# Triangular inverse of the RWKV recurrence: levels 1 to 5 over the 32 columns that each level changes

## What is computed

```python
def step(state, inp):
    r_t, w_t, k_t, v_t, kk_t, a_t = inp
    sk = jnp.einsum('bhij,bhj->bhi', state, kk_t)
    state = (state * w_t[:, :, None, :]
             - sk[..., None] * (kk_t * a_t)[:, :, None, :]
             + v_t[..., None] * k_t[:, :, None, :])
    y = jnp.einsum('bhij,bhj->bhi', state, r_t)
    return state, y
```

## Time and profile before

| | us |
|---|---|
| median of 3 runs | 3304.61 |
| the runs | 3301.97 to 3306.84 |
| the profiled execution | 3303.65 |
| its span, first to last instruction | 3301.9 |
| the stretch of the recurrence's levels in it | 1830.9 to 2411 |
| TensorE busy, whole span | 2822.2 (85%) |
| VectorE busy | 1513.9 (46%) |
| GpSimd busy | 1480.1 (45%) |
| ScalarE busy | 912.5 (28%) |

### The profile page before, as it was taken

The page is one execution under the profiler, slowest core; times in us unless marked ns, Lnnn a source line. Parts: engine busy times, 40 slices in busy tenths (PEclk is TensorE's granted clock), DMA queues, the critical chain, the costliest instruction groups (busy, mean ns, idle before and its releaser), DMA issues. The chain is left out here.

```text
span 3301.9 us, 59409 instructions
## 1 busy us (share of the span) xinstructions
PE 2822.2 (85%) x25224; PEld 2310.6 (70%) x25224; DVE 1513.9 (46%) x1839; ACT 912.5 (28%) x1616; POOL 1480.1 (45%) x817
## 2 busy tenths in 40 slices
PE   2788889999999994999644888888839999999999
PEld 1565667888888872777423778888738788878887
DVE  6744655655443445222342555555532544434434
ACT  2434433222222212222232333333322422222221
POOL 2533244444444442555442566555615544444443
PEclk9889989999999996999867999999969999999999
DMA  6512252545333320555324111111133232333233
GB/s 219 178 51 64 58 166 83 199 159 191 106 95 97 96 80 29 125 133 127 96 64 99 54 54 48 48 60 51 38 84 90 83 99 93 102 90 101 90 102 121
DMA packets 207762, 323.85 MB, mean 98 GB/s; under 512 B 126112, under 2 KB 126240, under 8 KB 207520
## 3 DMA queue, kind: packets, MB, share of 16 engines
q1 hardware_dynamic: 107680, 295.12, 29.1%
q10 hardware_dynamic: 99840, 25.17, 3.4%
HBM read 285.71 MB, written 33.55 MB: 97 GB/s over the span
## 5 line engine op out<-in xcount | busy, mean ns | idle before, releaser
L652 POOL TENSOR_TENSOR wl<-w,wh 128x1024 fp32r<-128x1024 f32 x320 | 782.2, 2450 | 1142.9 <-ACT wh L688 1142.6
L213 PE MATMUL ps<-hi,wh 128*128 128x512 f32 x1824 | 729.7, 400 | 58.7 <-POOL wl L652 43.9
L214 PE MATMUL ps<-lo,wh 128*128 128x512 f32 x1824 | 716.5, 393 | 0.0
L215 PE MATMUL ps<-hi,wl 128*128 128x512 f32 x1824 | 716.3, 393 | 0.0
L688 ACT ACTIVATE wh<-w 128x1024 fp32r<-128x1024 f32 x320 | 338.1, 1058 | 728.6 <-DMA w<-in_ffn_w_in 551.2
L899 DVE SCALAR_TENSOR_TENSOR xt<-ps,mod,xt 128x512 f32<-128x512 f32 x384 | 286.4, 750 | 429.8 <-PE ps L215 429.8
L213 PEld LDWEIGHTS ps<-hi,wh 128*128 128x128 f32 x1824 | 346.5, 190 | 144.5 <-POOL wl L652 44.1
L215 PEld LDWEIGHTS ps<-hi,wl 128*128 128x128 f32 x1824 | 346.1, 190 | 74.2
L214 PEld LDWEIGHTS ps<-lo,wh 128*128 128x128 f32 x1824 | 346.6, 190 | 73.4 <-issue 3.3
L213 PE MATMUL ps<-act_hi,wh 128*128 128x512 f32 x704 | 278.9, 396 | 11.4 <-DVE act_lo L908 10.2
L215 PE MATMUL ps<-act_hi,wl 128*128 128x512 f32 x704 | 277.7, 394 | 0.0
(11 more groups left out here) (214 smaller groups left out, 4537.6 us busy)
## 6 DMA issues: line engine op xcount, KB each, us to landing
w<-in_ffn_w_in SPq DMA_DIRECT2D x176, 512.0 KB, 3.7
piece<-in_ada_w SPq DMA_DIRECT2D x96, 512.0 KB, 4.8
w<-in_ffn_w_out SPq DMA_DIRECT2D x88, 512.0 KB, 3.6
w_raw<-in_w_rkv SPq DMA_DIRECT2D x48, 512.0 KB, 4.0
scratch<-stage ACTq DMA_DIRECT2D x96, 256.0 KB, 2.4
w<-in_wqk SPq DMA_DIRECT2D x20, 512.0 KB, 5.1
xt<-in_xT SPq DMA_DIRECT2D x4, 2048.0 KB, 12.1
w<-in_attn_w_out SPq DMA_DIRECT2D x16, 512.0 KB, 3.7
```

Source lines behind the costliest of these rows:

```text
L213: pe.matmul(out, w_hi(k), x_hi(k), start=first and k == 0, stop=False)
L214: pe.matmul(out, w_hi(k), x_lo(k), start=False, stop=False)
L215: ins = pe.matmul(out, w_lo(k), x_hi(k), start=False, stop=last and k == kc - 1)
L652: pool.tensor_tensor(wl[n % NW][:, :, :], wr[n % NW][:, :, :], wh[n % NW][:, :, :].bitcast(F32), ALU.subtract).then_inc(*wlo.up)
```

## The change

At level l with n = LEVELS[l], the product of `level_x` changes only the even blocks of n columns of each 64 (`blocks(.., l, 0)`), and the transpose only the odd ones (`blocks(.., l, 1)`): 32 columns either way. The moving operand, the output of each product, the sum and the two copies of levels 1 to 5 now go over these 32 columns. The stationary operands stay 64 x 64. The number of instructions in the levels and their order on each engine stay the same. Runs of neighbouring columns are 2 long at level 1, then 4, 8, 16 and 32.

So that the odd columns of `one_plus_x` are right without being written, each level has a tile of its own, filled with the identity once before the first period. Level 0 stays full and writes its sum to `inv`, where level 1 reads it.

```diff
-                wx, tinv = st("one_plus_x"), st("inv")
+                wx, tinv = [None] + [st(f"one_plus_x{l}") for l in range(1, len(LEVELS))], st("inv")
...
+                def blocks(x, l, odd):
+
+                    return x.rearrange("p a (g t n) -> p a g t n", t=2, n=LEVELS[l])[:, :, :, odd, :]
+
+                def merged(x):
+
+                    return x.rearrange("p a g n -> p (a g) n")
...
                             if l < NL - 1:
-                                act.activation(tinv[:, pairs, :], quarter(q), ACT.Copy)
-                            act.activation(inv[b][:, pairs, :], quarter(2 + q), ACT.Copy).then_inc(*g["t_done"].up)
+                                act.activation(merged(blocks(tinv[:, pairs, :], l, 0)), merged(blocks(quarter(q), l, 0)), ACT.Copy)
+                            act.activation(merged(blocks(inv[b][:, pairs, :], l, 1)), merged(blocks(quarter(2 + q), l, 1)), ACT.Copy).then_inc(*g["t_done"].up)
...
-                                    ins = pe.matmul(quarter(q)[hs, j, :], ntm[l % 2][hs, jj, :],
-                                                    idst[hs] if l == 0 else (wx if l == 1 else tinv)[hs, jj, :], start=True, stop=True)
+                                    if l == 0:
+                                        ins = pe.matmul(quarter(q)[hs, j, :], ntm[0][hs, jj, :], idst[hs], start=True, stop=True)
+                                    else:
+                                        ins = pe.matmul(blocks(quarter(q), l, 0)[hs, j], ntm[l % 2][hs, jj, :],
+                                                        blocks(tinv, l, 0)[hs, jj], start=True, stop=True)
...
                                     if l < NL - 1:
-                                        pe.matmul(quarter(q)[hs, j, :], inv[b][hs, jj, :], wx[hs, jj, :], start=True, stop=True)
+                                        pe.matmul(blocks(quarter(q), l, 0)[hs, j], inv[b][hs, jj, :], blocks(wx[l], l, 0)[hs, jj],
+                                                  start=True, stop=True)
...
-                                    ins = pe.matmul(quarter(2 + q)[hs, j, :], wx[hs, jj, :], inv[b][hs, jj, :],
+                                    ins = pe.matmul(blocks(quarter(2 + q), l, 1)[hs, j], wx[l][hs, jj, :], blocks(inv[b], l, 1)[hs, jj],
                                                     start=True, stop=True)
...
-                            dve.tensor_tensor(wx[:, pairs, :], quarter(q), idst.unsqueeze(1).to_broadcast([P, QP, CHUNK]),
-                                              ALU.add).then_inc(*g["w_done"].up)
+                            one = idst.unsqueeze(1).to_broadcast([P, QP, CHUNK])
+                            if l == 0:
+                                dve.tensor_tensor(tinv[:, pairs, :], quarter(q), one, ALU.add).then_inc(*g["w_done"].up)
+                            else:
+                                dve.tensor_tensor(blocks(wx[l][:, pairs, :], l, 0), blocks(quarter(q), l, 0), blocks(one, l, 0),
+                                                  ALU.add).then_inc(*g["w_done"].up)
...
                         dve.wait_ge(*g["zeros"].at(1))
+                        for x in wx[1:]:
+                            dve.tensor_copy(x[:, :, :], idst.unsqueeze(1).to_broadcast(W8)).then_inc(*g["wx_set"].up)
+                        dve.wait_ge(*g["wx_set"].at(NL - 1))
                         dve.wait_ge(*reset_in.at(1))
```

More of the change, by code:

```diff
@@ L94 @@
 wkv_s_done wkv_y_done_w wkv_m_step wkv_yc_done wkv_ysq_done wkv_var_done wkv_yrt_done wkv_yrn_done
-wkv_ybd_done wkv_yf_done wkv_z1_done wkv_bias_done wkv_z_step wkv_zeros g_in0*16 g_in1*16
+wkv_ybd_done wkv_yf_done wkv_z1_done wkv_bias_done wkv_z_step wkv_zeros wkv_wx_set g_in0*16 g_in1*16
 chunk_used0 chunk_used1 post_done0 post_done1 z_stored*16 z_in0*16 z_in1*16 z_hi z_lo stored*16
@@ L1318, in wkv_phase @@
                          "m_step yc_done ysq_done var_done yrt_done yrn_done ybd_done yf_done z1_done bias_done z_step "
-                         "zeros").split()
+                         "zeros wx_set").split()
                 g = {n: sig("wkv_" + n, 16 if n in ("tiles_in", "v_in") else 1) for n in names}
```

## The result

The changed kernel takes 3330.77 us (median of 4 runs, 3328.69 to 3332.42), against 3303.67 for the kernel before in the same comparison: ratio 1.0081, 95% interval 1.0063 to 1.0098. It is slower by 27 us. The forecast was 3298.6, the range 3288 to 3306.5.

The account below looks back on a forecast made before the run. TensorE's path with its waits for VectorE and GpSimd was taken to bound the recurrence; 0.303 us a period over 14 chunks (4.2), plus 0.7 and 1.1 for chunks 0 and 15, saved 6.0 us: 3298.6 us, range 3288 to 3306.5.

Parts of the forecast that it names:

- What bounds the kernel: Recurrence, TensorE 87% busy: the path of the 37.49 us period holds two VectorE sums and no ScalarE copy.
- the two sums that were named: VectorE's sums of levels 3 and 5, on the path: gains of 0.138 and 0.165 us a period.
- Part 1, the pace of TensorE: Matmuls of levels 1 to 5: a pair stays at 0.0587 us with 32 moving columns; only a batch's end 27 ns earlier.
- Part 2, the sums: VectorE sums of levels 1 to 5: each saves 0.138 us, ten a period, two of them on the path.
- Part 3, the copies: ScalarE copies, eighteen a period: each saves 0.107 us, counting only where a period lacks the work that hides them.
- Part 4, the fill: Filling tiles at the start: five VectorE copies, 3.5 us at most, hidden in 6.5 us of DMA wait, costing nothing.
- The sum: Whole recurrence: 4.2 us saved in chunks 1 to 14, 0.7 in chunk 0, 1.1 in chunk 15, total 6.0 us.
- the last rival: Recurrence: clock falls to 1.2 GHz as fewer columns move; a third of the stretch costs some 100 us; chance 0.03.

Follow-up runs that it names:

- e5: Changed kernel with all 64 columns in the products of levels 1 to 5, in jumping order (even blocks, then odd): 3304.06 us, ratio 1.0001.
- e12: As e10 (32 columns, waits filled), but the filling at level 3 is two matmuls of 128 x 192 for 128 x 256: 3299.65 us, ratio 0.9982.
- e10: Changed kernel, 32 columns, with unread matmuls filling TensorE's waits at levels 1, 2 and 3: 3301.79 us, ratio 0.9995.
- e11: As e10, same filling at levels 1, 2 and 3, but all 64 columns in the products: 3302.19 us, ratio 0.9999.
- e1: Changed kernel with all 64 columns in the products of levels 1 to 5, sums and copies at 32: 3302.07 us, ratio 0.9995.
- e9: Changed kernel with 64 columns in the products and 96 extra elements summed ahead of each sum, restoring the old period: 3303.28 us, ratio 0.9999.
- e7: Changed kernel with 64 columns in the products and unread matmuls filling the waits ahead of levels 1 and 2: 3300.01 us, ratio 0.9987.
- e3: Changed kernel with all 64 columns in the products of level 1 alone, levels 2 to 5 at 32: 3311.99 us, ratio 1.002.
- e6: Changed kernel, 32 columns, with unread matmuls filling the waits ahead of levels 1 and 2: 3315.17 us, ratio 1.0033.
- e2: Changed kernel, 32 columns, with 96 extra elements summed on VectorE ahead of each sum, restoring the old period: 3317.64 us, ratio 1.0048.
- e8: Kernel before the change, with unread matmuls filling the waits ahead of levels 1 and 2: 3304.26 us, ratio 1.0000.

## Why the prediction was wrong

- *What bounds the kernel*: right for a period at full clock. Ordinary periods take 37.17 us for the 37.19 forecast, through the two sums that were named: t3 starts 0.13 us earlier behind `state_products`, and `gram` k 0.16 earlier behind x5. Only the wait ahead of `gram` k was misread, forecast to shrink to 0.35 and measured at 0.54, since t5 ahead of it moved by about the same 0.16.
- *Part 1, the pace of TensorE*: right in an undisturbed period. Batches of 16 narrowed instructions start 0.46 to 0.47 us apart, 0.058 to 0.059 a pair, as forecast; in e5 jumps cost nothing. The Trainium skill ("Advanced Engine Details and Errata", "PSUM Cachelines") states that any non-contiguous PSUM pattern slows matmuls, beside asking that every two consecutive elements be neighbours. The first does not show here, neither at runs of 2 columns (1.15 us in e5) nor longer; the second was kept in every run and is not tested.
- *Part 2, the sums*: L1801 takes 282 ns for the 276 forecast. *Part 3, the copies*: 275 and 280 ns for 272 to 278. *Part 4, the fill*: hidden, and 1.77 us long for a bound of 3.5.
- *The sum*: 4.9 of the 6.0 us were for chunks 0 to 14. With the clock up, e12, the kernel of the forecast but for the filling, gives 5.7 us less over the levels, 0.3 in each period from chunk 1 on, as forecast, and 1.4 in chunk 0 (0.7 forecast). Part of the 1.4 is luck that the sum did not have, the order of VectorE and GpSimd shown under e10 and e11. In its median e12 is 4.4 us below the kernel before.
- *The step that failed* is that the sum took the granted clock as 1.00 in every period after the change too, and put its fall at nothing outside the last rival, "the clock falls, as fewer columns move", with a chance of 0.03. I read the 1.00 of the earlier trace rows as a state with room to spare, although the same rows showed TensorE stopping for 1.86 us in every period. It had none: e1 shows that 0.3 us off the period are enough, with every column still moving. In its place the runs showed a clock at half for 82 of the 573 us of the levels, which made them 19.9 us longer where 4.9 less were forecast. The rival's price was wrong too, "some 100 us": it took a third of the stretch for this, and a fall costs half its length less what the waits behind it give back, 4.2 us for the two of a slow period at 32 columns and 0.3 for the one at 64.
- The mechanism that I named for it was half of it. Shown by the pairs of runs: the moment at which the waits come (e1 against e9, at 64 columns); the waits themselves (e1 against e7, the changed kernel against e12); the number of columns, which makes a fall behind mask 1 10.2 us for 3.4 (the changed kernel against e1 and e3) and lets a 0.80 us wait start one (e3 and e6 against e1). What decides whether a given wait brings a fall stays open (in e1 the same wait brings none in chunks 2, 3 and 6); so does why e2 differs from run to run by 17 us.
- The Trainium skill ("TensorE: Matmul & The Clock Gate", section "Loop structure matters more than you think") ties a cold clock to loop nests in which long waits stand between the matmuls. In these traces one loop nest is at either level, and falls begin behind waits of 1.85 and of 0.80 us; where the two differ, the measurement decides.

## What to carry to other kernels

A granted clock of 1.00 in a stretch where TensorE stops again and again (here for 1.85, 1.33 and 0.80 us in each period) can be lost by a small change: before thinning out its matmuls or shortening a period, allow for a fall in the forecast, and read the clock stretch by stretch in the profile afterwards. Here, halving the moving columns of a small matmul whose weights stay 64 columns wide gained nothing in pace and made the falls longer. Where a wait cannot be removed, matmuls that nobody reads can hold the clock up: fitted into the wait they cost nothing here (e7, e8, e12), 0.2 us too long they cost 0.2 us a period (e10, e11).

## What the runs showed of the hardware

- With 64 x 64 weights in 32 bits and two heads side by side, a pair of instructions takes 0.058 to 0.059 us with 64 moving columns and with 32 alike; with 128 it takes 0.110.
- Runs of 2 neighbouring columns in the moving operand and in PSUM cost nothing (1.15 us for 32 instructions at level 1 in e5 and before). VectorE and ScalarE take 282 and 275 to 280 ns for 128 elements in runs of 2 to 32.
- At the lower level a batch of 16 narrowed instructions took 1.04 us for 0.66.
- Falls of the clock in chunks 0 to 14 lasted 3.4, 10.2 or 13.7 us. One and the same kernel with 32 columns (e2) had a mean clock of 0.951 in one execution and 0.944 in another (3310 to 3327 us).
- A multiply of 128 x 512 on VectorE and one on GpSimd that start within 0.04 us of each other do not run side by side at full pace: the second takes 1.78 for 0.69 us (VectorE, e11) or 1.79 for 1.27 (GpSimd, e10).
